# Idle products of the identity in TensorE's waits: expert routing and final stage of a backbone layer

## What is computed

```python
def hier_moe(h, p):
    lg = (h @ p['w_rg'] + p['b_rg']).astype(f32)
    g_sel = jnp.argmax(lg, axis=-1)
    le = (h @ p['w_re'] + p['b_re']).astype(f32).reshape(bsz, t, N_GROUPS, E_PER_GROUP)
    ...
    top_v, top_i = lax.top_k(le_sel, TOP_K) 
    w_top = jax.nn.softmax(top_v, axis=-1) * p_grp
    ...
    hid = jax.nn.silu(jnp.einsum('btd,edf->btef', h, p['w_e1'])) * jnp.einsum('btd,edf->btef', h, p['w_e3'])
    return jnp.einsum('btef,efd->btd', hid * gate[..., None], p['w_e2'])

def trunk_layer(x, mod, p, init_state):
    ...
    mixed, final_state = token_mixer(h, p, init_state)
    x = layer_norm(DN_ALPHA * x + gate1 * mixed, p['ln1_g'], p['ln1_b'])
    h = layer_norm(x) * (1.0 + scale2) + shift2
    x = layer_norm(DN_ALPHA * x + gate2 * hier_moe(h, p), p['ln2_g'], p['ln2_b'])
```

## Time and profile before

| | us |
|---|---|
| median of 3 runs | 1548.74 |
| lowest and highest | 1546.18, 1552.29 |
| the profiled execution, its own time | 1550.23 |
| span of its instructions | 1548.5 |
| mean granted clock of TensorE | 0.942 of 2.4 GHz |
| PE busy | 1353.8 (87%) |
| DVE busy | 565.8 (37%) |

### The profile page before, as it was taken

The page is one execution under the profiler, slowest core; times in us unless marked ns, Lnnn a source line. Parts: engine busy times, 40 slices in busy tenths (PEclk is TensorE's granted clock), DMA queues, the critical chain, the costliest instruction groups (busy, mean ns, idle before and its releaser), DMA issues. The chain is left out here.

```text
span 1548.5 us, 15938 instructions
## 1 busy us (share of the span) xinstructions
PE 1353.8 (87%) x6158; PEld 787.8 (51%) x6158; DVE 565.8 (37%) x1291; ACT 292.6 (19%) x597; POOL 81.3 (5%) x139
## 2 busy tenths in 40 slices
PE   4999999779898999999999999999749878776864
PEld 2455555555667786677776555544523323332321
DVE  5231566496033334354454211119631111111118
ACT  2202443350322334111111000000101111111110
POOL 0000000000000000000000000011011111110100
PEclk9999999889998999999999999999859988998987
DMA  9432323112011010121111253130179999998923
GB/s 378 159 136 109 109 95 150 55 35 89 6 33 60 6 60 1 63 69 41 41 42 41 102 177 104 59 133 41 76 327 404 424 422 424 423 422 357 376 79 134
DMA packets 57593, 242.37 MB, mean 157 GB/s; under 512 B 21518, under 2 KB 30286, under 8 KB 42670
## 3 DMA queue, kind: packets, MB, share of 16 engines
q1 hardware_dynamic: 51326, 229.79, 38.5%
q0 software_dynamic: 6048, 10.50, 1.8%
q10 hardware_dynamic: 144, 1.05, 0.2%
HBM read 233.54 MB, written 19.31 MB: 163 GB/s over the span
## 5 line engine op out<-in xcount | busy, mean ns | idle before, releaser
L2547 PE MATMUL bank<-ew,xgT 128*64 128x512 f32 x672 | 163.3, 642 | 35.5 <-DMA ew<-in_experts 19.0
L501 PE MATMUL bank<-hT,ring 128*128 128x512 f32 x320 | 165.3, 598 | 0.0
L1647 PE MATMUL bank<-hT,w_ab 128*128 128x512 f32 x256 | 131.2, 594 | 0.8 <-issue 0.8
L2547 PEld LDWEIGHTS bank<-ew,xgT 128*64 128x64 f32 x672 | 59.2, 148 | 135.5 <-issue 135.3
L928 PE MATMUL bank<-hT,ring 128*128 128x512 f32 x192 | 98.6, 595 | 2.2 <-DVE yA L1445 2.2
L502 PEld LDWEIGHTS bank<-hT,ring 128*128 128x128 f32 x320 | 60.8, 190 | 76.5 <-issue 76.5
L2561 PE MATMUL bank<-ew,hidT 128*64 128x512 f32 x336 | 81.8, 630 | 12.6 <-issue 12.0
L1648 PEld LDWEIGHTS bank<-hT,w_ab 128*128 128x128 f32 x256 | 48.7, 190 | 61.2 <-issue 61.2
L2656 DVE SCALAR_TENSOR_TENSOR uh<-uh,bank 128x256 f32<-128x256 f32 x21 | 8.8, 421 | 192.6 <-ACT uh L2610 192.6
L2058 PE MATMUL bank<-w_out,mT 128*128 128x512 f32 x160 | 70.9, 604 | 2.2 <-PEq L1580 2.2
L1762 PE MATMUL bank<-hT,w_c 128*128 128x512 f32 x128 | 65.5, 594 | 0.0
(11 more groups left out here) (438 smaller groups left out, 2087.9 us busy)
## 6 DMA issues: line engine op xcount, KB each, us to landing
ew<-in_experts SPq DMA_DIRECT2D x41, 2048.0 KB, 19.6
ew<-in_experts SPq DMA_DIRECT2D x41, 1024.0 KB, 21.3
ring<-in_blocks SPq DMA_DIRECT2D x10, 2048.0 KB, 8.4
mhalf<-in_mods SPq DMA_DIRECT2D x16, 1024.0 KB, 5.0
w_ab<-in_merge SPq DMA_DIRECT2D x16, 768.0 KB, 4.4
mstage<-in_mods SPq DMA_DIRECT2D x3, 2048.0 KB, 18.4
w_c<-in_merge SPq DMA_DIRECT2D x8, 768.0 KB, 4.5
yt<-expert_rows SPq DMA_DIRECT2D x5, 1024.0 KB, 9.1
```

Source lines behind the costliest of these rows:

```text
L501: pe.matmul(lat[:, :], w, hT[:, k, P:T], start=(k == 0), stop=(k == KD - 1))
L1647: pe.matmul(bank[5][:, :], w[:, k, :], hT[:, k, P:T], start=(k == 0), stop=(k == KD - 1))
L2547: mm = pe.matmul(bank[2 + x % 2][hs, :], xgT[:, x % 2, k, hs], ew1[:, 2 * (x % 2) + h, 2 * DE * k:2 * DE * (k + 1)], start=(k == 0), stop= ...
```

## The change

A helper issues n plain fp32 products of the identity with itself into bank 7, which nobody reads. It is called on PE at seven places: in out, two ahead of turn 3, eleven ahead of turn 4 and three behind it; in route, 22 at the start, 30 behind the rank products and 40 behind the table's; in final, 40 at the start. No wait is added, and nothing else is changed.

```diff
+    def filler(pe, n):
+
+        for _ in range(n):
+            pe.matmul(bank[7][:, 0:P], ident, ident, start=True, stop=True)
+
...
                 if i >= 3:
                     logits(i - 3)
+                if i == NT:
+                    filler(pe, 2)
+                if i == NT + 1:
+                    filler(pe, 11)
                 if 0 <= i - 2 < NT:
                     turn(i - 2)
+                if i == NT + 1:
+                    filler(pe, 3)
...
         @block.tensor
         def _(pe):
+            filler(pe, 22)
             pe.wait_ge(v9.sem, v9.after("mall"))
...
             mm.then_inc(p9.step("rank"), 1)
+            filler(pe, 30)
             pe.wait_ge(v9.sem, v9.after("rhs2"))
...
             mm.then_inc(p9.step("tab"), 1)
+            filler(pe, 40)
...
         @block.tensor
         def _(pe):
+            filler(pe, 40)
             for t in range(NT):
                 pe.wait_ge(got_y[t], 16)
```

## The result

| | before | changed |
|---|---|---|
| median of 4 runs each, us | 1547.72 | 1559.30 |
| lowest and highest, us | 1546.18, 1552.29 | 1557.91, 1562.64 |
| the profiled execution, its own time, us | 1550.23 | 1562.64 |
| span, us | 1548.5 | 1560.8 |
| mean granted clock | 0.942 | 0.950 |

The change is slower: ratio 1.0067, interval 1.0047 to 1.0087. (The ratios are worked out from the single runs of both kernels and need not be the quotient of the medians, which is 1.0075 here.) A repetition in a later session gave 1.0082 (1.0065 to 1.0100; 1560.11 us over 6 runs, against 1548.72 over 17). The time lies inside the range, above the forecast of 1555.3. The ratio is on the "slower" side of the 0.5% bound, with an interval that reaches over it at first and no longer in the repetition, while "same" had the larger chance.

The account below looks back on a forecast made before the run. PE's chain bounds out, DVE leads route and final, DMA paces experts. Terms 1.6 + 0.3 + 5.1 - 3.6 + 0 + 3.2 = +6.6 us gave 1555.3 us on the median of 1548.74; range 1549.5 to 1561.5.

Parts of the forecast that it names:

- same: Outcome within 0.5% (7.7 us) of the kernel before; chance 0.58, against 0.38 for slower and 0.04 for faster.
- Forty behind the table: End of route: the forty delay PE's drain and so POOL's first copy of experts; +5.1 us, the main term.
- Gather gives back: Start of experts: the first gather, issued later, takes 5.9 us instead of 9.5; -3.6 us, ends -7.4 and 0.
- Out: Block out: no wait covers the eleven, clock falling weighed two to one; +1.6 us, ends -0.6 and +5.9.
- 22 at the start: Start of route: the 22 are mostly hidden in PE's wait of about 5.5 us; +0.3 us.
- Thirty behind rank: Route: 6.7 us of products hidden in a wait of 8.05; rank products at full clock free DVE's 1.16 us.
- First gather turn and product: Start of experts: PE idle over 5 us again beforehand, so as cold as before; 0 us.
- Forty in final: Start of final: the forty outlast PE's 5.0 us wait; +3.2 us, middle of +1.6 (full clock) and +4.8 (cold first).
- A: Rival: batches run cold, in out to the end or route's forty; about +4.5 on the sum, 1559.8 us; chance 0.20.
- B: Rival: route's late barrier is hidden, the gather landing about 1149.5 as before; near 1552 us; chance 0.15.
- C: Rival: clock stays up and fillers are free in out, route, first gather and final; -7.8, 1540.9 us; chance 0.05.
- The rule: Skill page's throttled-time estimate: the two cold stretches, 47.8 and 10.3 us, hold 29 us to regain, ending near 1520.

Follow-up runs that it names:

- no_tail: The change without the forty products behind the table's products in route; 1550.17 us, ratio to the kernel before 1.0014.
- tail_behind: The change with route's forty moved from behind the table to the start of experts, behind the barrier; 1549.52 us, ratio to the kernel before 1.0012.
- covered2: covered with seven more products behind the last logits and six behind the table; 1540.87 us, ratio to the kernel before 0.9953; run again 1541.93 us, 0.9957.
- fin_20: The change with twenty instead of forty products at the start of final; 1553.69 us, ratio to the kernel before 1.0040.
- covered3: covered2 with three and five more products in each extra unit, ahead of first product and hidden transposes; 1546.31 us, ratio to the kernel before 0.9983.
- covered4: covered3 without the 21 products behind the last product of experts; 1539.57 us, ratio to the kernel before 0.9946.
- covered: The change with eleven between turn 3 and logits 3, 35 behind rank, none behind table, 46 starting experts, 21 ending it, 20 in final; 1544.73 us.

## Why the prediction was right, and where it was short

**Forty behind the table, +5.1: right.** Route is 27.2 us against 22.1. The working (start of the table, price of a record, drain, release) held to 0.1 us: POOL's copy came 21.71 us after the first mask product, forecast 21.77. no_tail and tail_behind show the cause by both ways, leaving out and moving. PE's drain ended some 9 us after the last of the table's products, where I had said some 10.

**Gather gives back -3.6: mis-sized, it was -1.65 (-1.35 in the repetition).** It needed 7.9 us from issue to PE, in the kernels with a late issue 7.9 to 8.3, where I took 5.9. It was weighed from the quickest gather of experts, 6.9, and a scatter with nothing beside it, 2.1. The nearer row was its own: 9.5 among the weights.

**Out +1.6: mis-sized, +2.6.** The working had two cases, the clock falls at logits 3 (+2.7) and it doesn't (-0.6), weighed two to one. In every kernel with only the two ahead of turn 3 it fell (3.23 to 3.56 us for the 16 records), and the loss was that of the first case to 0.1 us. The idle time was 2.37 us instead of 2.87, and nothing in the rows had said that this difference would save the clock. The far end, cold to the end of the block (+5.9), did not come: the eleven were cold, the turn, the three and the last logits were not.

**22 at the start, +0.3: 0.** The clock was up, so full cover. **Thirty behind rank: hidden**, as said; DVE's wait for the ranks is gone: its read of them, at 1123.85, follows its own work at once.

**First gather turn and product, 0: right in kind.** +0.3 us; the clock had fallen in the 9.63 us ahead of it (0.50 from 1146.5), 1.97 us for the turn as before. Experts: DMA at 1.01, 253.9 us for 254.3, so DMA does set the pace there.

**Forty in final, +3.2: mis-sized, +4.5**, near the end given for "cold when it begins, 6.6 us" (+4.8). It was cold to 1515.2, and I had taken the middle between that and full clock although showed the clock down at that place. The first tile's 3.6 us at full clock came as said (3.7).

Together: 6.6 + 1.0 (out) + 2.0 (gather) + 1.3 (final) - 0.3 (the 22) + 0.3 (first unit) - 0.4 (experts) = 10.5, and the columns above give the same. All three large misses go the same way: each time I set a cost between two cases, and the dearer one was what the rows at that place showed (the clock down, a gather of 9.5 us). In out and final it came nearly so, and with it there the forecast would have been 1558.0. At the gather it would have overshot: 7.9 us lies between 5.9 and 9.5, and with 9.5 the forecast would have been 1561.6. With the three terms as measured it is 1559.6, and its sign slower.

The mechanism of the main term was right, and so was the sign of the terms of out, gather and final. That the time fell inside the range is owed to a range of 12 us and not to the sizes: the sum was 6.6 us where the columns say 10.5 and the medians 11.6.

**Not foreseen:** the extra units. Their time runs from 84 to 92 us over the kernels, 4 us apart for the same one. PE's own chain takes most of them, and their second products take 3.65 us at full clock and 5.35 when it has fallen; in some profiles a unit or two also wait for weights, 2.08 us in the changed one. No edit of the change touches them. Comparisons by one profile need this column taken out.

**The rivals.** A (batches run cold) holds in part: the eleven and final's first records were cold, the forty of route weren't, which was A's other half. The measured 1559.3 is nearest to A's price of 1559.8, but by chance: neither of the two events that made up that price happened, and the difference came from the gather, from final and from 1 us in out. B (late barrier hidden) is refuted by no_tail. C (fillers free, clock up) is refuted for the change; the point from which it decides, products that end with DVE, is what covered2 arranges by place rather than by price, and there the gains of C appear: rank and table -2.4 (forecast -2.2), first turn and product -2.7 (-2.7), first sum -1.4 (-2.3).

**The rule.** By the prediction's estimate from the Trainium skill ("TensorE: Matmul & The Clock Gate", Terms) 29 us were to be had. The runs don't agree: with 53 us of unbroken full clock covered2 regains 6.9 us, and more than half of the throttled time was PE's own waiting (busy 21.2 of 47.8 us). The change reduced the throttled time by some 27 us (47.8 to 20.5) and lost 11.

## What to carry to other kernels

Ask of every filler batch not what clock it buys but what ends it: ahead of a barrier or a drain its last record is waited for by all engines, and one instruction further on, behind the barrier, the same batch was free here. Price it cold when the row at that place is cold, and place it in a wait about as long as that price; it may outlast the wait by what the full clock then saves in the work behind it, and no more (2.4 us against 2.2 in fin_20). Then the gain is what PE's chains were late by, and not the throttled time. Take a stage table from several profiles before an edit is judged by one.

## Of the hardware, not expected

- A branch over code that is not executed cost PE's queue up to 2.3 us in the kernel before, hidden behind a scatter, and up to 3.0 us in covered3 (median 0.14); two long ones in a row (2.74 and 3.01 us) lie in the 6.9 us ahead of its next product.
- The clock fell in short waits: the extra units have waits of 0.98, 1.45 and 0.52 us between dense products, and it fell there in some units and not in others (second products of 5.35 us in two of covered2's five units, in all five of tail_behind's), with nothing in the code to tell them apart. With eight products more in these waits all ten second products of covered3 and covered4 took 3.65 us.
- The fall can come after the work has resumed: in the changed kernel PE's idle time of 2.37 us ended at 1105.17 with the clock still up, and it was down from 1105.6 on, though PE was busy throughout (0.50 to 1112.4).
- The last store of `h2` landed 4.4 to 5.0 us after its issue in all five profiles with the eleven ahead of logits 3 (covered to covered4), and 2.6 us after it in all nine others. In covered, with PE's chain shorter, block out ended with it. Why it lands late there is open.
